# First tokens of a hybrid encoder layer: value, query, key, output and key-query projections with the tokens stationary and 512-column half-row blocks

## The chip, the core and the metric

The kernel runs on one core of a Trainium2 chip. The metric is the device time of one launch in microseconds (us); lower is better. All arithmetic is float32.

## What is computed

One encoder layer over 640 tokens: 512 of one prompt and 8 sequences of 16 sample tokens. D_MODEL is 2048, 1024 channels go to a convolution branch, 16 heads of 64 to attention.

```python
h = rmsnorm(x, norm1_g) * (1 + sc1) + sh1
z = h @ w_in                                  # 2048 -> [GLU value | GLU gate | q | k | v]
u = za * sigmoid(zg)
y_conv = silu(layernorm(causal_dwconv([left, u], w_dw, b_dw)))
o = band_attention(q, k, v)
x = x + g1 * (concat([y_conv, o]) @ w_out)
h2 = rmsnorm(x, norm2_g) * (1 + sc2) + sh2
# PEER: 8 heads, 2 halves each of 128 sub-keys
q = (h2 @ w_pq).reshape(t, 8, 2, 128)
s = einsum('thpd,pnd->thpn', q, sub_keys)     # the "scores" of a head's two halves
sv, si = top_k(s, 16); ...                    # 16 experts for each token and head
u = take(u_experts, eidx);  vv = take(v_experts, eidx)
act = gelu(einsum('td,ted->te', h2, u))       # the "dots"
x = x + g2 * einsum('te,ted->td', g * act, vv)
y = rmsnorm(x, final_g)
```

k and v of the layer are outputs too, in rows of tokens.

## The kernel before

The 640 tokens are 5 tiles of 128. The first two (the "first tokens", `X`, 256 tokens) go ahead alone so that their expert rows can be gathered while the other three (`Y`, 384 tokens) are still in their projections and attention. Every engine has its own program, in the order written in the file; engines wait for each other by semaphores, so what stands behind a wait on an engine waits with it. Nothing is scheduled by a planner.

The stages, in order of time: the modulation vectors (`w_ada`), the GLU columns of all tokens with the depthwise convolution on VectorE (DVE), then for X alone the queries, values and keys (`columns`, L784, and `values_part`, L794), the LayerNorm of the convolution, X's attention (`first_scores`, `first_turn`, `first_weigh`), its output projection (`project_out`, L884), RMSNorm, its key queries and scores (`key_queries`, L913, `key_scores`, L903); then the same for Y from `half_columns` on; and at last the rest of the gathers and a dense product over the value table.

How X's projections are made before: q, k and the key queries have a 128-column block of the weights stationary and stream the 256 tokens (matmuls of 256 columns), so the result has channels on partitions, as attention and the scores want it. v and the output projection have 128 tokens stationary and stream 256 weight columns. Weights come in loads of 256 columns by all 2048 rows (2 MB, rows of 1 KB) into ring slots. ScalarE (ACT) copies each result out of PSUM (`keep_columns`, `keep_values`, L1170 and L1176). For the output k, the kept keys are turned back to token rows in two of the four `rows_out` steps that stand in X's attention loop. The queries are written over the region in which the modulation rows wait to be stored, so ACT waits for that store (`mod_saved`) first.

The kept keys `kT` lie where the convolution's result lies, so they can be copied out only after the 16 Silu operations (L1199) that read it.

What follows the scores: on DVE, `choose(g, k)` (L1662) is the 18-step top-16 selection of head g of a token tile (g = 8 t + h). It waits for the scores of its head. `step(n)` (L1829) is one dot: it waits for gathered row n, runs a multiply-and-sum over 128x2048 (L1853), and interleaves one step of the selection of a head ahead:

```python
for g in range(2):
    for k in range(18):
        choose(g, k)
steps(124)
# in step(n), after the dot, g, s = divmod(n, 16):
if g >= 1 and g + 1 < NG and s < 2 and g + 1 not in (16, 17):
    choose(g + 1, 16 + s)
if g + 2 < NG and g + 2 not in (16, 17):
    choose(g + 2, s)
```

So the first step of head 2's selection stands right behind dot 0, and before dot 1. GpSimd (POOL) issues the gathers (L659), 1 MB each, into four buffers; a buffer is free when its dot is done. After 124 dots DVE turns to Y's attention (first L1914), for which TensorE (PE) waits.

## Time and profile before

| | |
|---|---|
| median of 3 runs | 4143.94 us (4139.81 to 4146.38) |
| the profiled execution's own time | 4143.43 us |
| its span | 4141.7 us |
| mean granted TensorE clock | 0.936 |
| PE / DVE / ACT / POOL busy | 87% / 67% / 11% / 27% |
| bytes moved | 1401.90 MB, mean 338 GB/s |
| X's q, v, k (first matmul to attention) | 510.8 to 717.5 us |
| X's attention | 717.5 to 774.0 us |
| X's output projection | 774.0 to 884.7 us |
| X's key queries | 901.0 to 1050 us |
| first dot, end of the first 124 dots | 950.1, 1371.2 us |

A span runs from the first to the last instruction. Busy shares are averages over stages with different limits; below, single stages are read. A float32 matmul appears in the trace as two records, so "x32" is 16 matmuls.

### The profile page before, as it was taken

What the parts mean: (1) busy time and instruction counts of PE and PEld (TensorE: products, weight loads), DVE (VectorE), ACT (ScalarE), POOL (GpSimd) and SP (SyncE); (2) the same over time, 40 slices, a digit from 0 to 9 for tenths busy, and PEclk for the clock granted to TensorE, in tenths of its full rate; (3) what the DMA queues carried; (4) which work ended last, traced back from release to release, by engine and by line L of the source; (5) the groups of instructions that cost most, each with busy time, mean ns of one, the idle gap of its engine ahead of it and who ended that gap; (6) DMA issues with size and microseconds to landing.
All of it is one profiled execution on the core that took longest, in us unless ns stands there. A gap on an engine that the chain in (4) does not pass through costs nothing.

```text
span 4141.7 us, 34885 instructions
## 1 busy us (share of the span) xinstructions
PE 3599.9 (87%) x12495; PEld 2018.6 (49%) x12495; DVE 2781.5 (67%) x5036; ACT 444.5 (11%) x1084; POOL 1135.5 (27%) x862
## 2 busy tenths in 40 slices
PE   4699989987998689779689999999868999996992
PEld 0466667776553564356534444444353444442441
DVE  2128871227787995679976676676798676655677
ACT  1100002210000230010800000000071000000000
POOL 1100000105554443345043222222404322221233
PEclk8799999998999679889899999999989999998996
DMA  9978743449999999989299999999929999999997
GB/s 351 230 236 259 245 139 130 147 144 380 403 402 413 367 357 335 366 331 397 110 376 417 421 420 409 421 418 421 401 89 374 417 421 421 419 420 397 421 409 304
DMA packets 377072, 1401.90 MB, mean 338 GB/s; under 512 B 22416, under 2 KB 187480, under 8 KB 239653
## 3 DMA queue, kind: packets, MB, share of 16 engines
q0 software_dynamic: 116784, 831.77, 50.4%
q1 hardware_dynamic: 259552, 563.91, 36.9%
q10 hardware_dynamic: 576, 4.19, 0.2%
q8 instruction: 87, 1.43, 0.1%
q14 instruction: 73, 0.60, 0.0%
HBM read 1369.87 MB, written 31.42 MB: 338 GB/s over the span
## 4 chain that ended last, share of the span: by engine, by line
DMA 46%; PE 26%; DVE 12%; issue 11%; POOL 3%; ACT 1%; another core or an unknown queue 0%; SPq 0%; DVEq 0%; POOLq 0%; ACTq 0%
DMA R<-in_u_experts,MS 32%; PE bank L763 10%; DMA R<-in_v_experts,MS 8%; PE bank L945 4%; PE bank L952 3%; DVE R L1763 3%; POOL R L659 3%; PE bank L891 3%; DMA R<-in_w_ada 2%; DVE R L1969 2%; DVE R L1853 1%; PE bank L802 1%; DMA R<-in_w_out 1%; PE bank L717 1%; DVE R L1762 1%
## 5 line engine op out<-in xcount | busy, mean ns | idle before, releaser
L659 POOL DMA_INDIRECT R<-in_u_experts,MS x640 | 931.1, 1455 | 1759.5 <-DVE MS L1853 1475.6
L1853 DVE CUSTOM_DVE_ANT_0 R<-R 128x2048 f32<-128x2048 f32 x368 | 844.4, 2295 | 416.8 <-DMA R<-in_u_experts,MS 404.8
L1118 PE MATMUL bank<-R,RB 128*128 128x512 f32 x2304 | 1019.0, 600 | 75.8 <-DMA R<-in_v_experts 75.7
L1118 PE MATMUL bank<-RB 128*128 128x512 f32 x1792 | 778.2, 592 | 0.0
L1118 PEld LDWEIGHTS bank<-R,RB 128*128 128x128 f32 x2304 | 440.6, 192 | 644.2 <-issue 550.6
L1853 DVE CUSTOM_DVE_ANT_0 R<-R,RB 128x2048 f32<-128x2048 f32 x272 | 622.2, 2287 | 117.5 <-DMA R<-in_u_experts,MS 116.3
L763 PE MATMUL bank<-RB,R 128*128 128x256 f32 (+1 forms) x2048 | 514.0, 412 | 51.4 <-DMA R<-in_w_pq 26.1
L1118 PEld LDWEIGHTS bank<-RB 128*128 128x128 f32 x1792 | 340.5, 190 | 428.6 <-issue 428.6
L763 PEld LDWEIGHTS bank<-RB,R 128*128 128x128 f32 x2048 | 393.1, 193 | 165.7 <-issue 33.9
L1969 DVE SCALAR_TENSOR_TENSOR R<-R,MS 128x2048 f32<-128x2048 f32 x128 | 301.3, 2354 | 183.3 <-DMA R<-in_v_experts,MS 182.0
L945 PE MATMUL bank<-RB,R 128*128 128x384 f32 x1024 | 338.1, 491 | 13.9 <-DMA R<-in_w_in 11.4
L952 PE MATMUL bank<-R,RB 128*128 128x512 f32 x576 | 257.9, 610 | 17.7 <-DMA R<-in_w_out 10.7
L945 PEld LDWEIGHTS bank<-RB,R 128*128 128x128 f32 x1024 | 194.4, 192 | 149.7 <-DMA R<-in_w_in 12.8
L659 POOL DMA_INDIRECT R<-in_v_experts,MS x128 | 154.9, 1210 | 357.6 <-DVE R L1969 328.0
L952 PEld LDWEIGHTS bank<-R,RB 128*128 128x128 f32 x576 | 112.3, 196 | 162.0 <-issue 139.8
L1107 PE MATMUL bank<-R 128*128 128x128 f32 x1024 | 143.8, 292 | 49.1 <-DVE R L1763 22.2
L1546 DVE SCALAR_TENSOR_TENSOR RB<-RB,MS 128x512 f32<-128x512 f32 x240 | 175.8, 732 | 0.0
L694 PE MATMUL bank<-MS,RB 128*128 128x128 f32 (+4 forms) x497 | 84.8, 325 | 87.9 <-DVE RB L1636 21.7
L1107 PEld LDWEIGHTS bank<-R 128*128 128x128 f32 x1024 | 127.4, 198 | 65.9 <-DVE R L1763 45.0
L1465 DVE TENSOR_TENSOR RB<-bank,RB 9x256 f32<-9x256 f32 x128 | 53.5, 418 | 153.4 <-PE bank L717 149.4
L1763 DVE TENSOR_SCALAR R<-MS 128x128 f32<-128x128 f32 x512 | 150.8, 332 | 8.5 <-PE bank L1107 8.5
L694 PEld LDWEIGHTS bank<-MS,RB 128*128 128x128 f32 (+4 forms) x497 | 68.4, 177 | 101.6 <-issue 38.2
(295 smaller groups left out, 2326.7 us busy)
## 6 DMA issues: line engine op xcount, KB each, us to landing
R<-in_v_experts SPq DMA_DIRECT2D x144, 1024.0 KB, 9.1
RB<-in_v_experts SPq DMA_DIRECT2D x112, 1024.0 KB, 9.1
R<-in_w_ada SPq DMA_DIRECT2D x48, 2048.0 KB, 12.8
R<-in_w_in SPq DMA_DIRECT2D x32, 2048.0 KB, 18.5
R<-in_w_out SPq DMA_DIRECT2D x16, 2048.0 KB, 11.5
R<-in_w_pq SPq DMA_DIRECT2D x16, 2048.0 KB, 17.1
R<-in_u_experts,MS POOLq DMA_INDIRECT x640, 11.5
RB<-in_x_prompt POOLq DMA_DIRECT2D x6, 1024.0 KB, 15.0
```

The lines of the kernel that those rows point to most:

```text
L659: pool.indirect_dma_start(dst, None, table, bass.IndirectOffsetOnAxis(ap=expert[T_ % 2][:, c:c + 1], axis=0)).then_inc(signal, 16)
L694: return pe.transpose(out, in_, ident[0:k, 0:k])
L763: m = pe.matmul(PB[2 * par + i][:, 0:src.shape[-1]], w, src[:, k], start=(k == 0), stop=(k == KT - 1))
L891: m = pe.matmul(PB[v % 4][:, 0:BW], src[:, k, t * P:(t + 1) * P], ring[:, j % 2, k, :], start=(k == 0), stop=(k == KT - 1))
L945: m = pe.matmul(PB[bank][:, 0:NY], wide[:, half, i, c * P:(c + 1) * P], src[:, 8 * half + i], start=(half + i == 0), stop=(half + i == 8))
L952: m = pe.matmul(PB[bank][:, :], src[:, 8 * half + i, t * P:(t + 1) * P], wide[:, half, i, :], start=(half + i == 0), stop=(half + i == 8))
L1107: m = pe.matmul(PB[n % 4][:, k * P:(k + 1) * P], oneh[n % 4][:, 1, k], oneh[n % 4][:, 0, k], start=True, stop=True)
L1118: x = pe.matmul(PB[4 * h + q][:, :], W[:, i, h * P:(h + 1) * P], vring[slot][:, q * PW:(q + 1) * PW], start=(i == 0), stop=(i == NKEY - 1))
L1546: ch.mark(STT(out=oP, in0=iP, scalar=w, in1=oP, op0=ALU.mult, op1=ALU.add))
L1763: m = TS(oneh[n % 4][:, 0, k], iota_row, turned[t % 2][:, 0, c:c + 1], turned[t % 2][:, 2, c:c + 1], ALU.is_equal, ALU.mult)
L1853: V.tensor_tensor_reduce(u, u, x, 1.0, 0.0, ALU.mult, ALU.add, dots[t % 2][:, h * TOPK + s:h * TOPK + s + 1]).then_inc(dots_done, 1)
L1969: STT(out=acc, in0=ux[p % NU], scalar=weight[TP][:, p:p + 1], in1=acc, op0=ALU.mult, op1=ALU.add).then_inc(v_used, 1)
```

## The change

X's five projections all get the form that Y's values have already (`half_rows`): 128 tokens stationary, 512 weight columns streamed, weights in half-row loads (1024 rows by 512 columns, again 2 MB, rows of 2 KB). A block of 512 columns takes two loads: both token tiles run on the first, then both on the second. There are `first_rows` for q, v and k, an inline loop for the output and `first_key_queries` for the key queries.

- v comes first, then q, then k. ACT keeps v without waiting for `mod_saved`.
- q and k now come out as token rows, so k needs no turning for its output: the two `rows_out` of k are gone and POOL stores the rows from where ACT put them. q and k are turned to channels by PE (16 transposes each) and copied again by ACT (`turned_rows`). k's turned copies stand behind the 16 Silu.
- The key queries come out as token rows, 2 heads (4 halves) to a 512-column block; they are copied, turned two halves at a time (`turn_queries2`), copied, and scored (`head_scores`). Each load is released half a block at a time.

```diff
@@ SP: loads @@
-            for j in range(NRING):
-                sp.wait_ge(z_done, 16 + 2 * (j + 1))
-                load("w_in", j, 4 * CC + j * BW)
+            x_cols = [(4, 2, 3)[m // 4] * CC + (m // 2 % 2) * PW for m in range(12)]
...
+            for m in range(4, 12):
+                if m % 2 == 0:
+                    sp.wait_ge(w_used, (m - 4) // 2 + 1)
+                else:
+                    sp.wait_ge(z_done, 16 + 2 * ((m - 4) // 2 + 1))
+                load_x_half(m, "w_in", m % 4, x_cols[m])
...
-            for m in range(NPH):
-                if m < 2:
-                    sp.wait_ge(o_done, 14 + 2 * m)
...
-                    sp.wait_ge(q_done, 2 * m - 2)
-                load_pq(m)
+            for m in range(8):
+                if m == 0:
+                    sp.wait_ge(w_used, 10)
+                elif m == 1:
+                    sp.wait_ge(o_done, 8)
+                elif m % 2 == 0:
+                    sp.wait_ge(w_used, 10 + m // 2)
+                else:
+                    sp.wait_ge(q_done, 4 * (m // 2))
+                sp.dma_start(wide[:, m % 2], wv["w_pq"][:, (m % 2) * 8:(m % 2) * 8 + 8, m // 2 * PW:(m // 2 + 1) * PW]).then_inc(w_q[m % 2], 16)
@@ PE: q, v, k @@
-            columns(16, hTX, 4)
-            values_part(24, hTX, 0, TX)
+            for m in range(2):
+                for half in range(2):
+                    first_rows(m, half)
+            first_rows(2, 0)
+            first_rows(2, 1)
+            first_rows(3, 0)
+            pe.wait_ge(mod_free, 4 + NM)
+            turn_queries(0)
+            first_rows(3, 1)
             pe.wait_ge(s_const, 2)
-            pe.wait_ge(mod_free, 4 + NM)
             pe.wait_ge(s_conv, 1)
             channel_sum(4, lambda c: conv_out[:, c], None, None).then_inc(s_mean, 1)
-            values_part(24, hTX, 1, TX)
+            first_rows(4, 0)
+            turn_queries(1)
+            first_rows(4, 1)
+            pe.wait_ge(s_tE, 4)
             channel_sum(6, lambda c: ysq[:, c % 2], s_ysq, s_ysq_used)
-            values_part(24, hTX, 2, TX)
-            values_part(24, hTX, 3, TX)
-            columns(32, hTX, 4)
+            first_rows(5, 0)
+            first_rows(5, 1)
...
-                if h in (3, 6, 9, 12):
+                if h in (3, 6):
                     rows_out(h // 3 - 1)
@@ PE: key queries @@
+            def head_scores(m):
+                for h in range(2):
+                    n = 2 * m + h
+                    pe.wait_ge(q_read, 2 * (n + 1))
+                    if n >= 2:
+                        pe.wait_ge(s_se, 2 * (n - 1))
+                    for t in range(TX):
+                        for p in range(2):
+                            x = pe.matmul(PB[6 + h][:, (2 * t + p) * P:(2 * t + p + 1) * P], q2h[:, h, p, t], skT[:, p],
+                                          start=True, stop=True)
+                    x.then_inc(s_s, 2)
+
+            def first_key_queries():
+                for m in range(4):
+                    for half in range(2):
+                        pe.wait_ge(w_q[half], 16 * (m + 1))
+                        if half == 0 and m >= 2:
+                            pe.wait_ge(s_rE, 2 * (m - 1))
+                        for t in range(TX):
+                            x = half_rows(h2TX, half, half, t, (2 * m + t) % 4)
+                            if half:
+                                x.then_inc(q_done, 2)
+                            elif t == TX - 1:
+                                x.then_inc(w_used, 1)
+                        if half == 0 and m >= 2:
+                            turn_queries2(m - 1)
+                    if m == 0:
+                        turn_queries2(0)
+                        head_scores(0)
+                    elif m >= 2:
+                        head_scores(m - 1)
+                turn_queries2(3)
+                head_scores(3)
@@ ACT @@
+            act.wait_ge(s_u, 8)
+            for v in range(4):
+                keep_columns(16 + v, vst[v])
             act.wait_ge(mod_saved, 16)
...
+            for t in range(TX):
+                keep_columns(26 + t, ost[:, t, PW:2 * PW])
             for c in range(CT):
                 act.wait_ge(s_lnx, c + 1)
...
             act.wait_ge(s_cat, CT)
-            for c in range(CT):
-                keep_columns(32 + c, kT[:, c, 0:NX])
+            for u in range(4):
+                turned_rows(4 + u, kT[:, 4 * (u // 2):4 * (u // 2) + 4])
```

The other lines renumber semaphore counts. DVE's program is the same but for the residual of X, which now has 8 pairs of operations on 512 columns in place of 16 on 256.

PE at X's key queries, before. L763 is the projection (x32 is two 128-column blocks, both halves of one head), L909 the scores.

```order
L694 MATMUL bank<-MS,RB 128x128 x32
L763 MATMUL bank<-RB,R 128x256 x32
L909 MATMUL bank<-MS 128x128 x4
L763 MATMUL bank<-RB,R 128x256 x32
L909 MATMUL bank<-MS 128x128 x2
L763 MATMUL bank<-RB,R 128x256 x16
```

The same place in the changed kernel. L808 is `half_rows`, L715 a transpose, L966 the scores of two heads.

```order
L715 MATMUL bank<-MS,RB 128x128 x32
L808 MATMUL bank<-R,RB 128x512 x32
L715 MATMUL bank<-MS,RB 128x128 x8
L966 MATMUL bank<-MS 128x128 x8
L808 MATMUL bank<-R,RB 128x512 x48
L715 MATMUL bank<-MS,RB 128x128 x8
L808 MATMUL bank<-R,RB 128x512 x16
L966 MATMUL bank<-MS 128x128 x8
```

Before, a half's scores follow one block of 16 matmuls behind its projection. Now the scores of heads 2 and 3 follow 64 matmuls of 512 columns and 8 transposes behind those of heads 0 and 1.

ACT between the last squares of the LayerNorm and X's attention, before. L1199 is Silu (16 of them), L1170 the copies of k, L1220 the first exponential. The 14 further Silu rows, which alternate in the same way, are left out.

```order
L1176 ACTIVATE MS<-bank 128x256 x4
L1199 ACT_TABLE_LOAD
L1199 ACTIVATE RB<-RB,MS 128x256
L1199 ACTIVATE RB<-RB,MS 128x384
...
L1170 ACTIVATE RB<-bank 128x256 x8
L1220 ACT_TABLE_LOAD
```

The same piece now. L1236 copies k's rows (these two are its last block), L1275 is Silu, L1241 the turned copies.

```order
L1236 ACTIVATE RB<-bank 128x512 x2
L1275 ACT_TABLE_LOAD
L1275 ACTIVATE RB<-RB,MS 128x256
L1275 ACTIVATE RB<-RB,MS 128x384
...
L1241 ACTIVATE RB<-bank 128x4x128 x4
L1298 ACT_TABLE_LOAD
```

Before, Silu stood ahead of all eight copies of k and ran beside its matmuls. Now it stands behind the copy of k's last block, and the turned copies, for which attention waits, behind Silu.

## Rows read from the trace of the kernel before

**Rows 1.** Timeline of PE, 500 to 720 us: start, us, engine, line, [idle before <-releaser].

```profile
510.83 14.08 PE L763 MATMUL bank<-RB,R 128*128 128x256 f32 x64
...
543.75 43.83 PE L763 MATMUL bank<-RB,R 128*128 128x256 f32 x192 [18.84 <-ACT RB L1170]
...
601.24 1.02 PE L810 MATMUL bank<-RB,MS 128*128 128x512 f32 x2
...
609.89 13.98 PE L802 MATMUL bank<-R,RB 128*128 128x256 f32 x64
...
717.54 0.71 PE L850 MATMUL bank<-RB 64*128 64x256 f32 x4 [0.56 <-ACT RB L1170]
```

**Rows 2.** Timeline of ACT, 500 to 960 us.

```profile
543.23 0.66 ACT L1170 ACTIVATE RB<-bank 128x256 f32<-128x256 f32 x2 [35.09 <-DMA mod_scratch<-RB]
...
662.16 1.28 ACT L1199 ACT_TABLE_LOAD   x1
...
663.46 8.82 ACT L1199 ACTIVATE RB<-RB,MS 128x256 f32<-128x256 f32 x16
...
898.85 2.06 ACT L1259 ACTIVATE RB<-bank 128x512 f32<-128x512 f32 x4 [2.55 <-PE bank L694]
```

**Rows 3.** Timeline of DVE, 608 to 620 us.

```profile
610.09 0.69 DVE L1571 TENSOR_TENSOR RB<-RB,bank 128x512 f32<-128x512 f32 x1 [16.58 <-PE bank L811]
```

**Rows 4.** Timeline of PE in X's attention and at the output projection.

```profile
738.49 0.70 PE L850 MATMUL bank<-RB 64*128 64x256 f32 x2
...
742.25 0.70 PE L850 MATMUL bank<-RB 64*128 64x256 f32 x2
...
745.14 0.70 PE L850 MATMUL bank<-RB 64*128 64x256 f32 x2
...
773.98 110.75 PE L891 MATMUL bank<-R,RB 128*128 128x256 f32 x512 [0.52 <-issue]
```

**Rows 5.** Timeline of PE in Y's values: 24 matmuls of 512 columns.

```profile
1311.33 20.87 PE L952 MATMUL bank<-R,RB 128*128 128x512 f32 x48 [1.26 <-DMA R<-in_w_in]
```

**Rows 6.** Timeline of PE, 880 to 1400 us: X's key queries, Y's attention.

```profile
900.97 14.08 PE L763 MATMUL bank<-RB,R 128*128 128x256 f32 x64 [0.84 <-ACT RB L1259]
...
990.28 9.62 PE L763 MATMUL bank<-RB,R 128*128 128x256 f32 x32 [15.67 <-DMA R<-in_w_pq]
...
1373.00 3.78 PE L1007 MATMUL bank<-RB 64*128 64x128 f32 x16 [37.04 <-DVE RB L1914]
```

**Rows 7.** Timeline of DVE, 880 to 1100 us: residual, selection, first dots.

```profile
884.76 0.42 DVE L1620 TENSOR_TENSOR MS<-bank,R 128x256 f32<-128x256 f32 x1 [6.02 <-PE bank L891]
...
938.41 0.49 DVE L1683 MAX8 MS<-RB 128x8 f32<-128x128 f32 x2 [2.99 <-ACT RB L1265]
...
950.07 2.28 DVE L1853 CUSTOM_DVE_ANT_0 R<-R,RB 128x2048 f32<-128x2048 f32 x1
...
953.12 0.49 DVE L1683 MAX8 MS<-RB 128x8 f32<-128x128 f32 x2 [0.76 <-ACT RB L1265]
...
953.52 2.27 DVE L1853 CUSTOM_DVE_ANT_0 R<-R,RB 128x2048 f32<-128x2048 f32 x1
```

**Rows 8.** L393 (w_pq loads), issue at 944.8, then issue at 959.5: time to landing.

```profile
DMA to landing us min/median/max: 12.0/12.0/12.0
...
DMA to landing us min/median/max: 30.7/30.7/30.7
```

**Rows 9.** L332 (weight loads), issues from 420 to 900 us: time to landing.

```profile
DMA to landing us min/median/max: 7.9/8.5/18.3
```

**Rows 10.** Stretches: us, PE PEld DVE ACT POOL busy, PEclk, DMA share, GB/s.

```profile
953.50:1371.20 417.70, 334.57 (x1066) 202.31 (x1064) 337.37 (x545) 24.37 (x50) 229.54 (x123) 0.91 1.01 402
...
2100.00:2900.00 800.00, 783.92 (x1807) 344.32 (x1806) 554.83 (x892) 6.06 (x7) 226.44 (x201) 0.99 1.01 418
```

**Rows 11.** Waits of DVE, 953.5 to 1371.2 us: total, times, longest.

```profile
DVE R L1853 <- DMA R<-in_u_experts,MS: 77.8, 86, 4.3
```

**Rows 12.** L659 (gathers) in Y's attention, 1378 to 1567 us: time to landing.

```profile
DMA to landing us min/median/max: 6.0/9.0/10.3
```

More of the change, by code:

```diff
@@ L381, in _ @@
                 first_bias(h)
-            for j in range(2):
-                sp.wait_ge(z_done, 32 + 2 * (j + 1))
-                load("w_out", j, j * BW)
+            sp.wait_ge(w_used, 5)
+            load_x_half(0, "w_out", 0, 0)
+            sp.wait_ge(z_done, 26)
+            load_x_half(1, "w_out", 1, 0)
             for h in range(4, NH):
@@ L929, in _ @@
             pe.wait_ge(s_cat, CT)
             pe.wait_ge(pv_read, NH)
-            for j in range(8):
-                project_out(0, j, catX, TX)
-            pe.wait_ge(o_free, 4 + 16)
+            for j in range(4):
+                for half in range(2):
+                    weights_in(half)
+                    for t in range(TX):
+                        v = TX * j + t
+                        if half == 0:
+                            pe.wait_ge(o_free, v + 1)
+                        m = half_rows(catX, half, half, t, v % 4)
+                        if half:
+                            m.then_inc(o_done, 1)
+                        elif t == TX - 1:
+                            m.then_inc(w_used, 1)
@@ L934, in _ @@
+            pe.wait_ge(o_free, 4 + 8)
             pe.wait_ge(s_sq, T + TX)
@@ L947, in half_columns @@
                 return m
-            def half_rows(src, half, t, bank):
-                for i in range(8):
-                    m = pe.matmul(PB[bank][:, :], src[:, 8 * half + i, t * P:(t + 1) * P], wide[:, half, i, :],
-                                  start=(half + i == 0), stop=(half + i == 8))
-                return m
             for b in range(4):
@@ L974, in _ @@
                     for t in range(TY):
-                        m = half_rows(hTY, half, t, TY * j + t)
+                        m = half_rows(hTY, half, half, t, TY * j + t)
                         if half:
@@ L1265, in keep_scores, with keep_rows2, keep_turned2, keep_head_scores @@
                 A(dst[:, 0:tiles, n], PB[4 + 2 * b][:, 0:tiles * P].rearrange("p (t n) -> p t n", t=tiles), ACT.Copy).then_inc(s_se, 1)
+            def keep_rows2(m):
+                for t in range(TX):
+                    act.wait_ge(q_done, 4 * m + 2 * t + 2)
+                    if m >= 2:
+                        act.wait_ge(s_tT, 8 + 2 * (m - 1))
+                    A(qrows[:, m % 2, t], PB[(2 * m + t) % 4][:, :], ACT.Copy).then_inc(s_rE, 1)
+            def keep_turned2(m):
+                for h in range(2):
+                    n = 2 * m + h
+                    act.wait_ge(s_tT, 8 + n + 1)
+                    if n >= 2:
+                        act.wait_ge(s_s, 2 * (n - 1))
+                    A(q2h[:, h], PB[4 + h][:, :].rearrange("p (i t n) -> p i t n", i=2, t=TX), ACT.Copy).then_inc(q_read, 2)
+            def keep_head_scores(m):
+                for h in range(2):
+                    n = 2 * m + h
+                    act.wait_ge(s_s, 2 * (n + 1))
+                    A(SX[:, :, 2 * n:2 * n + 2], PB[6 + h][:, :].rearrange("p (t i n) -> p t i n", t=TX, i=2), ACT.Copy).then_inc(s_se, 2)
+            def keep_first_queries():
+                keep_rows2(0)
+                keep_turned2(0)
+                keep_head_scores(0)
+                keep_rows2(1)
+                for m in range(1, 4):
+                    keep_turned2(m)
+                    if m < 3:
+                        keep_rows2(m + 1)
+                    keep_head_scores(m)
             def keep_queries(G, dst, tiles):
@@ L1640, in _ @@
             for i in range(4):
-                dve.wait_ge(s_vst[i], 16 * 2)
-            for v in range(8 * TX):
+                dve.wait_ge(s_vst[i], 16)
+            for v in range(4 * TX):
                 j, t = divmod(v, TX)
```

263 lines of the change are left out of this document (141 added, 122 removed).

## The prediction

> **What bounds the kernel now.** I read the chain of waits first. From X's key queries on it runs over DVE and the gathers for 400 us, then Y's attention, then to the end. So two questions matter: when do the dots start, and how fast do they run. The timeline of DVE gives the start: dot 0 at 950.07, then head 2's selection at 953.12, dot 1 at 953.52 [rows 7]. The stretch of dots 1 to 123 takes 417.7 us at 402 GB/s, with a DMA share of 1.01 [rows 10]. DVE waits for gathers for only 77.8 us of it [rows 11]; without them it would take 339.9 us. PE waits 37.04 us for DVE at Y's attention [rows 6]: up to there PE has slack and DVE has none. All later stages follow DVE's 124th dot one to one: 48 dots stand in Y's attention, where they never wait, and what follows is in the same order as before. So the sum is the shift of the start of Y's attention on DVE, now 1371.2.
>
> Before the dots, 510 to 950 us, PE bounds. It idles 18.84 us at 524.9 [rows 1], since ACT waits until 543.23 for the modulation store [rows 2].
>
> **Streaming.** 512 columns bring PE nothing: 24 matmuls of 512 take 20.87 us, 0.870 each [rows 5]; 256 matmuls of 256 take 110.75, 0.433 each [rows 4]. Half the matmuls at twice the price. A half-row load is 16 matmuls (two tiles), 13.91 us. X's q, v and k have 12 of these, the output projection 8, the key queries 8.
>
> **From 510.83 to X's attention.** v runs first and is not held, so the 18.84 us go. PE: v 4 x 13.91 to 566.5; q's first three 41.7 to 608.2; 8 transposes (0.87, which is what a head with a turning group costs above one without, 3.76 - 2.89 [rows 4]); q's last 13.91 to 623.0. The convolution is done by then: DVE had been idle for 16.58 us at 610.09, since 593.5 [rows 3]. Channel sum 8.65 (601.24 to 609.89 [rows 1]) to 631.7; k's first block with 8 transposes 28.7 to 660.4; second channel sum 8.65 to 669.0; k's second block 27.8 to 696.9. A weight load lands in 8.5 us (at most 18.3) [rows 9] and has 13.9 us or more; the one issued at 507 beside two others is needed at 524.7, as before. I cost the loads at nothing; their cover is those 13.9 us.
>
> Here ACT is late next. Behind k's last copy (0.6) come the Silu table and the 16 Silu, 1.28 + 8.82, which lay beside k's matmuls before [rows 2], then 4 turned copies, 2.06 for four of that size [rows 2]. PE's 16 transposes lie beside them. Attention can start at 696.9 + 12.8 = 709.7, where it started at 717.54 [rows 1]: -7.8 us. The 18.84 us are given back in part to three terms: 12.8 behind k, 1.7 for q's transposes, and 0.09 for each load.
>
> **X's attention** loses two turning groups: -1.7. PE comes to it after 13 us with no matmul but the transposes. After an idle of 15.67 us, 16 key-query matmuls took 9.62 us instead of 7.04 [rows 6]. Attention is not PE's to set, so between 0 and +2.6 I take +1. The output projection then starts at 765.4 (before 773.98). It takes 111.3 for 110.75, to 876.7. The last residual has two operations on 512 columns, 0.69 each [rows 3], where it had 0.42 [rows 7]: +0.5. Norm, transposes and copies are unchanged, 884.73 to 900.97, 16.24. Key queries start at 893.5, 7.5 us early.
>
> **Scores of heads 0 and 1.** Block 0 takes 27.8 + 0.3 to 921.6; copy 0.6, transposes 0.9, copies, scores and copies some 2.3. Both heads' scores are there at about 925. Selection 0 is free at once. One selection takes 11.7 us (938.41 to 950.07 [rows 7]); two take it to 948.3. Dot 0 starts about 2 us earlier than before.
>
> **Scores of heads 2 and 3: the new wait.** Selection 2 stands between dot 0 and dot 1. Its scores come behind 64 matmuls of 512, no longer behind 32 of 256. PE goes on at 924.3; block 1 to 952.1; the first half of block 2 needs a load issued at 938 beside the first four gathers. The nearest rows are 12.0 us to landing (few gathers about) and 30.7 (the dots at full rate) [rows 8]. Against 13.9 that is a stall of 0 to 17. Since DVE issues only one gather more before it waits, it is nearest to the first; four gathers and the load are 6.3 MB, at 402 GB/s 15.7 us, so I take +2. The Trainium skill, "DMA: Bandwidth & Descriptors", Queues, rings and completion order, says an engine takes turns between its queues packet by packet. By that the load would have half the rate and land in 10.4 us, and the sum would be 2 lower. Block 2 then ends at 954.1 + 13.9 + 0.9 + 13.9 = 982.8; scores and copies 1.2: 984.0. Dot 1 starts at 984.4, where it started at 953.5: +30.9 us.
>
> **What of that comes back.** While DVE waits, only PE's loads move. At dot 1 before, the key-query loads for blocks 5 to 7 and a rest of the fourth were still to come, 3.3; now only the last one has, since PE has run on without its stalls of 15.67 and so on [rows 6]. 2.3 loads of 2.1 MB are 4.8 MB; the stretch had 417.7 x 402 = 167.9 MB to move, now 163.1. At 402 GB/s that is 405.7 us, against 417.7: -12. Dot 124 ends at 1390.1. The bounds: at the 418 GB/s of the later stage with 8 KB rows [rows 10] it is 390.2, a shift of +3.4; by DVE alone 339.9 [rows 11], if transfers were no bound at all. I take 402, since the same weight loads share this stretch; they end some 27 us earlier than before, but from there DVE's own 339.9 / 123 = 2.76 us a dot and up leaves little to catch up.
>
> PE's other gains do not count. It finishes Y's values some 27 us earlier, and waits for DVE 87 instead of 37.
>
> Sum: -7.8 - 0.7 (attention) + 0.6 + 0.5 brings the key queries 7.5 earlier; the start of dot 1 is +30.9; the stretch gives back 12: **+19 us**. On the profiled execution's 4143.4 that is 4162.4; it lies 0.5 below the median of the runs, so the forecast is 4162.5.
>
> **The rivals.**
>
> *A. The wait is mostly made up.* If the stretch can move 418 GB/s once DVE comes in refreshed and the weight loads thin out, the shift is +3.4, 4147. For it: the same engines do 418 later. Against: there all rows are 8 KB, here 17 weight loads (a fifth of the bytes) have rows of 1 or 2 KB. Chance 0.15.
>
> *B. More goes wrong ahead of the scores.* The load for block 2 lands like the 30.7 us one: 17 instead of 2, so +15 more; or ACT holds X's q copies, and the early 7.5 us are lost. Price +27 to +42: 4171 to 4185. Against: DVE is waiting, so no gathers crowd the load. Chance 0.11.
>
> *C. Faster.* The stretch is not bound by bytes, but by the loop of four buffers: landing, dot, issue. In Y's attention, with few weight loads about, gathers land in 9.0 us in the median [rows 12]. Then a loop is 9.0 + 2.3 for the dot + 0.9 for the issue, 12.2 us for four dots, 3.05 a dot; 123 of them take 375 us. Place: dots 1 to 123. From 984.4 they end at 1359.6, a shift of -11.6: 4132. It decides for faster once a dot takes under 3.07 us; before it took 3.40. For it: DVE waits in only 77.8 of 417.7 us. Against: a DMA share of 1.01, and the 9.0 us come from a stage with 48 dots in 195 us, a third fewer gathers in the air. The Trainium skill, same page, Where 436 GB/s comes from, has 435 GB/s as the ceiling; at that 163.1 MB would take 375 us, the same answer. No stretch here shows more than 418. Chance 0.09.
>
> That the change does not do what it says is excluded by the order: no engine schedules itself.
>
> **How the numbers follow.** The forecast (shift +9 to +27, 4152 to 4170) has 0.65, A 0.15, B 0.11, C 0.09. What a measurement of this kernel can tell from no change is 0.2%, 8.3 us: 4135.7 to 4152.2. Slower: 0.65 + 0.11 = 0.76; within: A, 0.15; faster: C, 0.09. Range 4146 to 4178: the forecast, most of A and half of B, 0.82.
>
> **What would show it.** Right: PE without the wait at 525; attention of X about 8 us earlier, with ACT's Silu right ahead of it; key queries near 893; the first step of selection 2 waiting about 31 us for ACT's score copy, with dot 0 near 948 and dot 1 near 984; hardly a stall for w_pq loads; PE's wait for DVE at Y's attention about 87 us; Y's attention at about 1390. Wrong: a wait ahead of selection 2 under 15 us, or dots 1 to 123 in under 395 us.

## The result and the profile after

The change makes the kernel slower, by 0.6 to 1%. Four runs of it have a median of 4189.91 us (4173.62 to 4196.73), four of the kernel before 4141.88 us (4139.69 to 4146.38): ratio 1.0097, 95% interval 1.0078 to 1.0117. The direction was forecast; the size was not, +48 us against the +19 of the forecast, and the result lies outside the range. Seven more runs of the same kernel in a later set have a median of 4172.19 us (4166.74 to 4187.92) against 4148.19: ratio 1.0062 (1.0039 to 1.0085), +24 us. So this kernel's own time varies by 30 us, and what it varies by is part of the answer. Two profiled executions of the changed kernel are read here: execution one, 4191.98 us, and execution two, 4169.90 us, from the later set.

Timeline of PE in execution one (columns as in [rows 1]):

```profile
512.76 96.40 PE L808 MATMUL bank<-R,RB 128*128 128x512 f32 x224
...
710.10 1.23 PE L894 MATMUL bank<-RB 64*128 64x256 f32 x4 [11.26 <-ACT RB L1241]
...
781.27 112.27 PE L808 MATMUL bank<-R,RB 128*128 128x512 f32 x256 [0.51 <-issue]
...
911.28 29.73 PE L808 MATMUL bank<-R,RB 128*128 128x512 f32 x64 [0.69 <-ACT RB L1337]
...
976.59 15.70 PE L808 MATMUL bank<-R,RB 128*128 128x512 f32 x32 [3.90 <-DMA R<-in_w_pq]
...
1418.68 3.78 PE L1073 MATMUL bank<-RB 64*128 64x128 f32 x16 [81.41 <-DVE RB L2024]
```

The wait of 18.84 us of [rows 1] is gone: 224 records follow one another from 512.76 on. X's attention starts 7.4 us earlier than before, but the output projection behind it starts 7.3 us later (before 773.98 [rows 4]). Y's attention starts 45.7 us later, after a wait for DVE of 81.41 instead of 37.04 us [rows 6].

ACT ahead of X's attention, the same execution:

```profile
697.13 0.60 ACT L1236 ACTIVATE RB<-bank 128x512 f32<-128x512 f32 x1 [6.27 <-PE bank L808]
697.74 1.28 ACT L1275 ACT_TABLE_LOAD   x1
699.04 8.82 ACT L1275 ACTIVATE RB<-RB,MS 128x256 f32<-128x256 f32 x16
707.89 2.07 ACT L1241 ACTIVATE RB<-bank 128x512 f32<-128x512 f32 x4
```

That is the 12.8 us of work the prediction put there. DVE, at the rows that answer to [rows 7]:

```profile
945.17 0.49 DVE L1793 MAX8 MS<-RB 128x8 f32<-128x128 f32 x2 [33.44 <-ACT RB L1364]
...
968.02 2.29 DVE L1963 CUSTOM_DVE_ANT_0 R<-R,RB 128x2048 f32<-128x2048 f32 x1
...
1008.63 0.49 DVE L1793 MAX8 MS<-RB 128x8 f32<-128x128 f32 x2 [38.31 <-ACT RB L1364]
1009.03 2.27 DVE L1963 CUSTOM_DVE_ANT_0 R<-R,RB 128x2048 f32<-128x2048 f32 x1
```

Head 2's selection waits 38.31 us for the score copy where it waited 0.76 us. Dots 1 to 123 and the attention of X as stretches (columns as in [rows 10]):

```profile
710.10:781.27 71.17, 65.11 (x192) 40.46 (x193) 21.48 (x127) 32.06 (x101) 8.93 (x16) 0.50 0.21 66
...
1009.03:1417.20 408.17, 296.48 (x854) 158.72 (x852) 336.90 (x547) 23.05 (x42) 219.81 (x122) 0.87 1.01 400
```

408.2 us at 400 GB/s are 163.3 MB, against 163.1 forecast. The new thing is in the first row: the granted clock is 0.50, its lower level (1.2 GHz), through all of X's attention. A head takes 3.97 us. In the kernel before only the third and fourth head start at that price, and from the fifth on a head takes 2.89 us (3.76 with a turning group). The starts of scores of the third, fourth and fifth head (the row of four records ahead of them is the first two heads, every further row one):

```profile
723.26 1.22 PE L850 MATMUL bank<-RB 64*128 64x256 f32 x2
...
727.24 1.22 PE L850 MATMUL bank<-RB 64*128 64x256 f32 x2
...
732.71 0.70 PE L850 MATMUL bank<-RB 64*128 64x256 f32 x2
```

Execution two of the changed kernel has the same 11.26 us wait ahead of attention as execution one, and yet:

```profile
708.45:764.47 56.02, 41.82 (x192) 27.55 (x193) 21.50 (x127) 32.07 (x101) 8.96 (x16) 0.85 0.26 83
988.60:1395.10 406.50, 295.62 (x854) 158.34 (x852) 336.82 (x547) 23.15 (x42) 226.60 (x122) 0.87 1.01 402
```

Here the clock came back at about 725 us, behind the first four heads, as in the kernel before at about 732 us. Attention takes 56.0 us, 15.2 fewer. The starts side by side, in us:

| | before | forecast | execution two | execution one |
|---|---|---|---|---|
| X's attention | 717.54 | 709.7 | 708.45 | 710.10 |
| X's output projection | 773.98 | 765.4 | 764.47 | 781.27 |
| key queries | 900.97 | 893.5 | 892.65 | 911.28 |
| selection 0 | 923.98 | 925 | 924.53 | 945.17 |
| dot 0 | 950.07 | 948.3 | 947.40 | 968.02 |
| dot 1 | 953.52 | 984.4 | 988.70 | 1009.03 |
| Y's attention on PE | 1373.00 | 1391.9 | 1396.58 | 1418.68 |
| span | 4141.7 | 4160.7 | 4168.1 | 4190.2 |

(1391.9 is the shift of 18.9 us on 1373.00, and 4160.7 is 4141.7 + 19.)

### The profile page after: what moved, and what is told of

Same layout as the page of the kernel before. It is cut to its first block, busy times and chain, and to the rows that moved or that the text cites. A ratio compares the mean times of both kernels' runs of the same rounds, so it can differ in the third digit from the quotient of the medians.

```text
span 4190.2 us, 33145 instructions
## 1 busy us (share of the span) xinstructions
PE 3625.8 (87%) x11647; PEld 1864.1 (44%) x11647; DVE 2777.6 (66%) x5020; ACT 446.5 (11%) x1069; POOL 1114.0 (27%) x858
## 4 chain that ended last, share of the span: by engine, by line
DMA 47%; PE 24%; issue 13%; DVE 11%; POOL 3%; ACT 1%; another core or an unknown queue 0%; SPq 0%; DVEq 0%; POOLq 0%; ACTq 0%
DMA R<-in_u_experts,MS 34%; PE bank L808 11%; DMA R<-in_v_experts,MS 8%; PE bank L784 7%; POOL R L680 3%; DVE R L1873 3%; DMA R<-in_w_ada 2%; DVE R L2079 2%; DVE R L1963 2%; PE bank L738 1%; DVE R L1872 1%; DMA R<-in_w_out 1%; PE bank L715 1%; PE bank L1073 0%; DMA R<-in_w_pq 0%
## 5 line engine op out<-in xcount | busy, mean ns | idle before, releaser
L680 POOL DMA_INDIRECT R<-in_u_experts,MS x640 | 910.4, 1422 | 1816.4 <-DVE MS L1963 1525.8
L1184 PE MATMUL bank<-R,RB 128*128 128x512 f32 x2304 | 1019.2, 600 | 81.0 <-DMA R<-in_v_experts 80.8
L1184 PEld LDWEIGHTS bank<-R,RB 128*128 128x128 f32 x2304 | 440.6, 192 | 649.6 <-issue 549.5
L808 PE MATMUL bank<-R,RB 128*128 128x512 f32 x1472 | 650.5, 604 | 27.8 <-DMA R<-in_w_in 13.9
L808 PEld LDWEIGHTS bank<-R,RB 128*128 128x128 f32 x1472 | 284.0, 194 | 385.9 <-issue 353.0
L784 PE MATMUL bank<-RB,R 128*128 128x256 f32 (+1 forms) x1024 | 282.3, 437 | 5.6 <-DVE RB L1625 5.6
L1018 PEld LDWEIGHTS bank<-RB,R 128*128 128x128 f32 x1024 | 194.4, 191 | 149.5 <-DMA R<-in_w_in 14.8
L784 PEld LDWEIGHTS bank<-RB,R 128*128 128x128 f32 x1024 | 194.8, 192 | 90.3 <-issue 13.6
L715 PE MATMUL bank<-MS,RB 128*128 128x128 f32 (+3 forms) x561 | 95.2, 322 | 96.3 <-DVE RB L1860 24.4
L715 PEld LDWEIGHTS bank<-MS,RB 128*128 128x128 f32 (+3 forms) x561 | 75.5, 173 | 117.2 <-issue 43.8
```

The source lines that it names most:

```text
L680: pool.indirect_dma_start(dst, None, table, bass.IndirectOffsetOnAxis(ap=expert[T_ % 2][:, c:c + 1], axis=0)).then_inc(signal, 16)
L715: return pe.transpose(out, in_, ident[0:k, 0:k])
L784: m = pe.matmul(PB[2 * par + i][:, 0:src.shape[-1]], w, src[:, k], start=(k == 0), stop=(k == KT - 1))
L808: m = pe.matmul(PB[bank][:, :], src[:, 8 * half + i, t * P:(t + 1) * P], wide[:, slot, i, :], start=(half + i == 0), stop=(half + i == 8))
L1018: m = pe.matmul(PB[bank][:, 0:NY], wide[:, half, i, c * P:(c + 1) * P], src[:, 8 * half + i], start=(half + i == 0), stop=(half + i == 8))
L1184: x = pe.matmul(PB[4 * h + q][:, :], W[:, i, h * P:(h + 1) * P], vring[slot][:, q * PW:(q + 1) * PW], start=(i == 0), stop=(i == NKEY - 1))
```

## The experiments

Two theories stood after the first trace. **One:** the score wait (64 matmuls of 512 ahead of the scores of heads 2 and 3) costs what was forecast, and the rest is the clock in X's attention. **Two:** the rest comes from the changed streaming or the loads in v, q, k and the output projection. All experiments edit the changed kernel, save the one that moves attention in the kernel before. They were run in three sets, each with its own runs of the kernel before, whose medians are 4147.47, 4148.19 and 4148.72 us. Every version has one profiled execution. Up to the end of X's attention the versions "key queries of before", "scores of block 1 at once" and "head 2's selection deferred" are the changed kernel unchanged.

**The key queries of before.** Only the key queries (with their loads, copies and scores) go back; v, q, k and the output projection stay as changed.

```diff
-            first_key_queries()
+            key_queries(0, h2TX, TX)
```

> The changed kernel with the key queries of X as they were before the change (weights stationary, 256-column loads, a head's scores one block behind), all else changed. Theory 1: the key queries start where they start now, 911, which is 10 us later than before the change, and from there everything runs as before: dot 0 near 960, dot 1 near 964, 26.7 us of stalls for w_pq loads, Y's attention near 1383, the kernel 10 us above the kernel before, 4152. So of the 48 us lost some 38 are the key queries' part. Rival: the key queries cost nothing by themselves, and the loss is all in the slow attention and what it shifts (17 us) and in contention: then the time stays above 4180.

Measured: 4148.55 us (4129.87 to 4162.79, 10 runs), ratio 0.9999 (0.9979 to 1.0019). Five runs lie at 4130 to 4145 and five at 4153 to 4163 us. The profiled one belongs to the second five, and shows the lower clock to the end of attention (us, PE busy, PEclk, DMA share, GB/s):

```profile
710.00:720.00 10.00, 6.01 (x21) 0.50 0.41 156
...
740.00:760.00 20.00, 19.88 (x57) 0.50 0.31 78
```

The forecast was 4152 us. So the loss on the median belongs to the key queries, and the first half of the change is worth nothing on the median: what it gains in half of the runs, it loses in the others, where the mean clock is lower (0.924 to 0.930, against 0.934 to 0.936). That all five kept the lower level through attention is read from one of them. Theory two falls.

**Scores of block 1 at once.** The queries of block 1 are turned and scored behind block 1 instead of behind the first half of block 2; ACT's copies move along.

```diff
-                        if half == 0 and m >= 2:
-                            turn_queries2(m - 1)
-                    if m == 0:
-                        turn_queries2(0)
-                        head_scores(0)
-                    elif m >= 2:
-                        head_scores(m - 1)
+                        if half == 0 and m == 3:
+                            turn_queries2(2)
+                    if m < 2:
+                        turn_queries2(m)
+                        head_scores(m)
+                    elif m == 3:
+                        head_scores(2)
```

> The changed kernel with the key queries of block 1 (heads 2 and 3) turned and scored right behind that block, as block 0's are, instead of one block later. Theory 1: DVE's wait ahead of head 2's selection (38.3 us) is a cost of the order alone. It falls to about 6 us, dot 1 starts about 32 us earlier (near 977 instead of 1009), and since fewer weight loads have been done by then, 9 to 12 us are given back in the stretch of dots 1 to 123; Y's attention starts 20 to 24 us earlier, and the kernel takes about 4168. Rival: the stretch is bound by bytes from the first dot on and all of the wait is made up, so that Y's attention starts at the same time within 5 us, and the kernel takes 4186 to 4191.

Measured: 4144.22 us (4134.86 to 4168.00, 10 runs), ratio 1.0001 (0.9979 to 1.0023), 28 us under the changed kernel's 4172.19. Seven runs lie at 4134.9 to 4145.0 us with clocks of 0.932 to 0.938, three at 4162.7 to 4168.0 with 0.924 to 0.928: two groups here too. DVE waits for head 2's scores (first row below) far less than 38.31 us:

```profile
955.25 0.49 DVE L1794 MAX8 MS<-RB 128x8 f32<-128x128 f32 x2 [6.49 <-ACT RB L1364]
```

On PE:

```profile
707.52 1.23 PE L894 MATMUL bank<-RB 64*128 64x256 f32 x4 [11.26 <-ACT RB L1241]
...
1368.45 3.78 PE L1073 MATMUL bank<-RB 64*128 64x128 f32 x16 [38.65 <-DVE RB L2025]
```

Y's attention starts 28.1 us earlier than in execution two (forecast 20 to 24 against execution one). Both executions had the recovered clock, and selection 0 starts within 0.9 us of the same time, so this is the price of where the scores stand.

**Head 2's selection deferred.** Nothing moves on PE; DVE no longer stands behind the wait.

```diff
+                if g == 0:
+                    if s >= 8:
+                        choose(2, 2 * s - 16)
+                        choose(2, 2 * s - 15)
-                if g + 2 < NG and g + 2 not in (16, 17):
+                elif g + 2 < NG and g + 2 not in (16, 17):
                     choose(g + 2, s)
```

> The changed kernel with one edit on DVE: the sixteen pieces of head 2's selection stand two by two behind dots 8 to 15 instead of one by one behind dots 0 to 15, so that dots 1 to 7 no longer stand behind its wait for the scores. Theory (the score wait stops the weight gathers through their buffers): selection 0 still starts some 21 us later than before, the scores of head 2 still come at about 1008 us in an execution with the low clock in attention, but dots 1 to 7 (3.3 us each) run in that wait, and the attention of Y starts some 20 to 24 us earlier than in the changed kernel: about 1396 us with the low clock in the first tokens' attention and 1380 us with the recovered one; median about 4167 us. Rival (the gathers are late by the start of selection 0 and 1 alone, or by another queue): Y's attention starts as late as in the changed kernel, median 4185 to 4190 us.

Measured: 4152.97 us (4140.40 to 4177.58, 10 runs), ratio 1.0018 (0.9997 to 1.0039). The expected median of 4167 us was reckoned from 4185; from the 4172.19 of the same set the gain is 19 us. The profiled execution had the lower clock throughout attention, as execution one had:

```profile
942.91 0.49 DVE L1793 MAX8 MS<-RB 128x8 f32<-128x128 f32 x2 [33.51 <-ACT RB L1364]
...
1007.97 0.49 DVE L1793 MAX8 MS<-RB 128x8 f32<-128x128 f32 x2 [14.31 <-ACT RB L1364]
```

```profile
1396.79 3.78 PE L1073 MATMUL bank<-RB 64*128 64x128 f32 x16 [60.53 <-DVE RB L2028]
```

The scores are as late as in execution one (1008.63), but the wait is 24.0 us shorter, and Y's attention starts 21.9 us earlier, 2.3 of which come from an earlier start of selection 0. So late scores cost less by themselves than through what stands behind them: the dots, and with them the buffers of the gathers.

**Silu first.** The 16 Silu go ahead of the copy of k's last block on ACT, so that PE's last 32 matmuls hide them.

```diff
-            for t in range(TX):
-                keep_columns(26 + t, ost[:, t, PW:2 * PW])
             for c in range(CT):
                 act.wait_ge(s_lnx, c + 1)
                 ...
                 m.then_inc(s_cat, 1)
+            for t in range(TX):
+                keep_columns(26 + t, ost[:, t, PW:2 * PW])
```

> The changed kernel with its 16 Silu on ACT moved ahead of the copy of k's last block, so that they run beside that block's matmuls. Two theories on X's attention, which took 71.2 us here (3.97 us a head) and 56.4 before (2.89 a head). Theory 1: TensorE's clock is at its lower level for the whole attention because PE stands idle for 11.3 us right ahead of it, while ACT does Silu. Then attention starts about 10 us earlier (700 instead of 710), a head takes 2.89 us again after the first few, and the output projection starts 24 to 26 us earlier, near 756; the kernel takes about 4165 us. Rival: the clock is low because attention has two turning groups less, whatever stands ahead of it. Then a head still takes 3.97, only the 10 us are won, and the kernel takes about 4181.

Measured: 4167.30 us (4150.19 to 4184.99, 8 runs), ratio 1.0054 (1.0034 to 1.0074). PE at the scores of the first four heads:

```profile
698.42 0.71 PE L894 MATMUL bank<-RB 64*128 64x256 f32 x4 [1.00 <-ACT RB L1241]
704.15 1.22 PE L894 MATMUL bank<-RB 64*128 64x256 f32 x2
708.12 1.22 PE L894 MATMUL bank<-RB 64*128 64x256 f32 x2
```

The wait of 11.26 us is 1.00. Y's attention starts at 1388.72, 7.9 us ahead of execution two's. But two of the eight runs still took 4184 and 4185 us, with mean granted clocks of 0.925 and 0.920 against 0.929 to 0.933 in the others. If these two kept the lower clock through attention (they have no profile), the idle ahead of attention is not what decides whether the clock comes back.

**The wait filled.** The same wait holds 26 matmuls of 256 columns (output used nowhere).

```diff
+            pe.wait_ge(z_free, 2 + 28)
+            for i in range(26):
+                pe.matmul(PB[0][:, 0:2 * P], ident, skT.rearrange("p h n -> p (h n)"), start=True, stop=True)
             pe.wait_ge(s_tE, 8)
```

> The changed kernel with 26 matmuls of 256 columns more, identity by the sub-keys into a free PSUM bank, in the 11.3 us in which PE waits for ACT ahead of X's attention; their result is not used. Theory 1 (the idle stretch drops TensorE's clock, and attention does not bring it back): attention starts at the same time within 1.5 us, takes 56 to 58 us instead of 71.2, and the kernel takes about 4176. Rival (attention's own light load keeps the clock low): 3.97 us a head as before, and the same time or 1 us more, 4191.

Measured: 4170.76 us (4164.59 to 4193.56, 5 runs), ratio 1.0069 (1.0040 to 1.0098). PE at the scores of the first three heads and of the fifth:

```profile
708.98 0.71 PE L897 MATMUL bank<-RB 64*128 64x256 f32 x4
...
714.73 1.22 PE L897 MATMUL bank<-RB 64*128 64x256 f32 x2
...
724.02 0.70 PE L897 MATMUL bank<-RB 64*128 64x256 f32 x2
```

PE enters attention at the full clock, which is at the lower level 5.8 us later and back at 724 us; Y's attention starts at 1395.82, as in execution two. One of the five runs, 4193.56 us at a clock of 0.923, looks like execution one. A busy PE ahead of attention buys nothing here: without the idle, the clock falls in the attention itself.

**The changed kernel once more**, for its spread.

> The changed kernel itself, unedited. What decides its spread: if the first tokens' attention runs its 16 heads either at the lower clock throughout (71 us) or with three heads only at it (55 us), the times fall into two groups about 16 us apart, near 4173 and near 4190 us, as the four runs so far have it (4173.6 against 4187.9 to 4196.7); the rival is one broad group. No change in the median of about 4185 us.

Measured: 4166.74, 4167.56, 4169.90, 4172.19, 4174.03, 4179.88 and 4187.92 us. The last, with the lowest clock (0.922), falls where execution one is. Of eleven runs, four lie at 4187.9 to 4196.7 us with clocks of 0.922 to 0.924, seven at 4166.7 to 4179.9 with 0.928 to 0.934. My expectation of a median of 4185 us missed: the first four runs had held three with the lower clock.

**More columns in attention.** Two matmuls of 256 columns more in ten of the 16 heads, where PE waits for DVE anyway.

```diff
+                if h == 9:
+                    pe.wait_ge(s_oE, 2)
+                if 1 <= h <= 2 or 9 <= h <= NH:
+                    for i in range(2):
+                        pe.matmul(PB[6][:, i * 256:i * 256 + 256], ident, skT.rearrange("p h n -> p (h n)"), start=True, stop=True)
                 if 1 <= h <= NH:
                     first_turn(h - 1)
```

> The changed kernel with two matmuls of 256 columns more in 10 of the 16 heads of the first tokens' attention, ahead of the turn for which TensorE waits 0.70 us a head at the full clock (their output is used nowhere). Theory (attention is so light on TensorE that the clock falls in it, and it comes back by chance): more columns bring the clock back after about three heads in all or nearly all executions, at little cost at the full clock, attention some 56 to 60 us, and the times lie in one group near 4173 us. Rival (the load has nothing to do with it): as many executions as without them stay at the lower clock, where each pair costs 0.87 us, 10 heads 8.7 us, so one group near 4198 us and another near 4175 us.

Measured: 4175.74 us (4173.28 to 4184.49, 6 runs), ratio 1.0063 (1.0042 to 1.0085): a single group 11 us wide. With four in eleven at the lower clock, six without one would come by chance 7 times in 100, so this alone does not settle it. The time does not tell it either: the profiled execution is the slowest, 4184.49 us, and yet its clock was back by the fifth head (724.85 us). Nor is the version faster: its median is 3.6 us above that of the changed kernel in the same set. (A pair is 0.87 us at the full clock, not at the lower one as I had written; a head with a pair takes 3.03 instead of 2.89 us.)

**The same columns with the key queries of before.**

> The changed kernel with the key queries of before, and the same extra matmuls in attention. Without them 5 of 10 executions lay at 4130 to 4145 us and 5 at 4153 to 4163 us. Theory: one group at 4132 to 4148 us, about 3 us above the lower group for the extra matmuls' own time. Rival: two groups as without them.

Measured: 4146.25 us (4138.47 to 4153.90, 11 runs), ratio 0.9995 (0.9985 to 1.0004). Of the ten runs without the columns five lay at 4152.6 us or above, of these eleven one (4153.90, at a clock of 0.934), with two more at 4151.5; the spread is 15 us instead of 33. Five of the eleven lie above the 4132 to 4148 us of the forecast. In the profiled execution the clock is back by the third head, at 716.5 us, a little short of full in places (0.94):

```profile
710.00:720.00 10.00, 7.65 (x27) 0.67 0.56 219
720.00:730.00 10.00, 8.07 (x43) 0.94 0.20 52
...
740.00:760.00 20.00, 20.00 (x101) 1.00 0.21 58
```

The median gains only 2.3 us, though: the group lies 9 us above the lower half of the version without the columns (mean 4137.4). The extra matmuls explain about 1.4 of them (ten heads by 0.14); the rest is not explained.

**The kernel before, attention moved.** 24 matmuls of 256 columns ahead of X's attention in the kernel before.

> The kernel before with 24 matmuls of 256 columns (0.216 us each, 5.2 us, TensorE busy, output used nowhere) ahead of the first tokens' attention, which moves it from 717.5 to about 722.7 us. Asked: is it the changed kernel's stage of v, q and k, or only the time at which attention begins, that lets the clock stay low in some executions? If it is only the phase: some executions of this one also keep the low clock through attention, two groups some 16 us apart, near 4149 and 4165 us. If it is the stage ahead: one group as for the kernel before, median about 4152 us, which is 4147 us and the 5 us added.

Measured: 4157.73 us (4150.93 to 4168.29, 11 runs), ratio 1.0020 (1.0009 to 1.0031).

```profile
717.90 10.60 PE L844 MATMUL bank<-MS 128*128 128x256 f32 x48 [0.56 <-ACT RB L1172]
728.42 0.71 PE L852 MATMUL bank<-RB 64*128 64x256 f32 x4
```

24 matmuls are 48 records of 0.22 us, so the shift was 10.9 us, not 5.2. The median went up by 9.0, which the shift accounts for. Four of the eleven runs lie at 4163 to 4168 us, 4 us above the next, but with clocks of 0.931 to 0.932, within the 0.929 to 0.938 of the kernel before. So moving attention in time shows no clear second group, and eleven runs do not exclude one; the profiled execution is the second shortest.

**All three moves, then with the columns.** Silu first, block 1's scores at once, head 2's selection deferred:

> The changed kernel with three edits together: Silu ahead of the copy of k's last block on ACT, block 1's queries turned and scored right behind block 1, and the deferral of head 2's selection. If the three waits are separate, their gains add as far as they stand on one path: selection 0 starts some 10 us earlier than before (about 913 us), and nothing waits in front of dot 1, so Y's attention starts about 1356 to 1362 us against 1373 before; median 4128 to 4138 us, faster than both kernels. Rival (the stage of dots is then bound by something that these edits do not move, such as the start of the weight gathers, or the low clock in attention returns in most executions): 4140 us or more.

Measured: 4141.07 us (4122.44 to 4157.12, 12 runs), ratio 0.9987 (0.9967 to 1.0008). DVE reaches dot 1 with no wait for scores, and Y's attention starts within the forecast 1356 to 1362:

```profile
1357.40 3.78 PE L1073 MATMUL bank<-RB 64*128 64x128 f32 x16 [50.76 <-DVE RB L2029]
```

The median missed by 3 us and falls on the rival's side (4140 or more): five of the twelve runs lie at 4150 to 4157 us, with clocks of 0.926 to 0.931. None of the five has a profile.

> The version with all three moves (Silu ahead of the copy of k's last block, block 1's scores right behind block 1, head 2's selection deferred) and the extra matmuls in 10 heads of the first tokens' attention (two of 256 columns each, output used nowhere). Theory (the extra columns keep the chip from leaving TensorE at the lower clock for the whole of attention): one group of times at 4125 to 4145 us, median about 4136 us, none near 4155 us, where 5 of 12 executions without the extra matmuls lay (4150 to 4157 us). Rival (the six executions with them that agreed did so by chance): the same two groups, a third or more of the executions at 4155 us and above, median 4143 us or more.

Measured: 4132.42 us (4119.55 to 4145.98, 7 runs), ratio 0.9964 (0.9950 to 0.9977). This version beats both kernels: 16 us under the kernel before. Against the version without the columns it is 9 us faster in the medians, though the intervals of the two ratios overlap. Its PE is at the full clock at the third head's scores (0.70 us, not 1.22; the fourth takes 0.80):

```profile
697.63 0.71 PE L894 MATMUL bank<-RB 64*128 64x256 f32 x4 [1.00 <-ACT RB L1246]
702.99 0.70 PE L894 MATMUL bank<-RB 64*128 64x256 f32 x2
...
1354.25 3.78 PE L1078 MATMUL bank<-RB 64*128 64x128 f32 x16 [27.69 <-DVE RB L2034]
```

Over the three versions with the columns, 24 runs, the times of each spread over 11, 15 and 26 us; the same versions without them spread over 30, 33 and 35 us, with 4 of 11, 5 of 10 and 5 of 12 runs in what looks like an upper group. The borders of these groups are drawn by eye (in the 26 us one run, 4145.98, stands 11 us above the next), and in the medians the columns are worth +3.6, -2.3 and -8.7 us.

**From selection 0 to Y's attention.** The distance between these two starts in the profiled executions leaves out all that the clock did in X's attention, and shows what the key queries, the selections and the dots take:

| | selection 0 | Y's attention on PE | between |
|---|---|---|---|
| kernel before | 923.98 | 1373.00 | 449.0 |
| kernel before, attention moved | 934.83 | 1383.24 | 448.4 |
| changed kernel, execution one | 945.17 | 1418.68 | 473.5 |
| changed kernel, execution two | 924.53 | 1396.58 | 472.1 |
| Silu first | 913.16 | 1388.72 | 475.6 |
| the wait filled | 923.78 | 1395.82 | 472.0 |
| more columns in attention | 928.89 | 1399.71 | 470.8 |
| key queries of before | 935.18 | 1377.35 | 442.2 |
| scores of block 1 at once | 923.63 | 1368.45 | 444.8 |
| head 2's selection deferred | 942.91 | 1396.79 | 453.9 |
| all three moves | 911.85 | 1357.40 | 445.6 |
| all three moves, with the columns | 914.55 | 1354.25 | 439.7 |

All five executions in which the key queries and the selection are those of the change lie at 471 to 476 us, whatever the clock did ahead of them, 22 to 27 above the kernel before. Moving block 1's scores takes all of that away, deferring the selection four fifths of it.

## Why the prediction was right and wrong

**Right: the start of X's attention.** The step "attention can start at 696.9 + 12.8 = 709.7" measured 710.10 and 708.45. The weight loads cost nothing, and the 12.8 us are ACT's last copy, Silu with its table, and the turned copies. With the Silu first the wait is 1.00 us.

**Wrong: "Attention is not PE's to set, so between 0 and +2.6 I take +1."** This term of the sum was mis-sized, and its upper bound was as well. It is the step that failed, by 15.5 us where the clock stays low. In execution two it holds (56.0 us, forecast 55.7). In execution one attention takes 71.2 us, 15.5 over the forecast. The reason given was false: at the lower clock the row 710.10:781.27 has PE busy for 65.11 of 71.17 us, so there it is PE's to set, at 3.97 us a head. [rows 4] has only rows at the full clock, and [rows 6] bounded one block of key queries. The price of a head at the lower level stood in the trace of before (3.98 us from 723.26 to 727.24). The bound had to be the 12 heads behind the first four by 1.08 us, 13 us, and some 2 us for a turning group and the last heads' turns and products: one execution in which the clock came back does not say that it must. With the 15.5 the sum is 4178, the upper end of the range.

That is still 12 us short of the median of 4189.91. Execution one's span ends 29.5 us behind the forecast: 20.2 are there at selection 0 (15.5 of them attention; the output projection takes 112.27 instead of 111.3, as the granted clock is still 0.72 from 780 to 790 us, and block 0 of the key queries 29.73 instead of 28.1), 4.5 more come at dot 1, 2.1 between dot 1 and Y's attention, and 2.7 behind it. Execution two is 7.4 behind the forecast, with nothing from attention.

**Right, somewhat short: the score wait.** "Dot 1 starts at 984.4" measured 988.70 in execution two. The wait ahead of head 2's selection, forecast at about 31 us, is 38.3 and 38.6. Of the 4.3 us, 2.2 are the stall for block 2's load (4.2 instead of the 2 taken) and 1.8 the half block behind it (15.70 instead of 13.9). The stall itself speaks against the shorter landing: the load was issued at 938.4 us and PE went on at 956.25, 17.9 us later (17.6 in execution one). The Trainium skill, "DMA: Bandwidth & Descriptors", Queues, rings and completion order, has an engine take turns between its queues packet by packet. From it the prediction took half the rate and an estimate of 10.4 us; this trace does not agree with the estimate, and is nearer to the 15.7 us that the load and the gathers beside it take one after the other. Two edits confirm the mechanism: scores moved, Y's attention 28 us earlier; selection deferred, 22 us earlier with scores as late as ever.

**Right: what comes back.** 405.7 us forecast for dots 1 to 123; 406.5 and 408.2 measured, at 402 and 400 GB/s. In execution two Y's attention is 23.6 us later than before, where the sum had 18.9.

**The rivals.** A (418 GB/s) and C (the loop of buffers) did not occur. B's price, 4171 to 4185, is the nearest of the three to what was measured, but that is luck: it rested on a stall of 17 us, which was 3.9 and 4.2, or on a loss of the early 7.5 us ahead of attention, and attention did start as early as forecast.

**The spread.** Of the seven runs at 4167 to 4180 us six lie within the range of 4146 to 4178. The four others don't, and the range had no case for them. What follows Y's attention adds its own: the distance from its start to the end is 2768.7 us before, 2771.5 in both executions of the changed kernel, and from 2759.7 to 2784.4 in the experiments, whose edits lie ahead of it. What moves it is not known, so a difference of some 10 us between two profiled executions should be read at Y's attention and not at the end.

**Open.** With v, q and k changed, the lower clock lasts through attention in a part of the runs. The kernel before shows no such group: of its 73 runs beside the experiments one is at 4166.6 us with a clock of 0.929, the others are at 4135.4 to 4160.1 us. The filled or removed wait and the moved start did not decide it. With the extra columns no run looks like execution one, which speaks for too little work for TensorE in attention, but this is argued and not shown. The change takes two turning groups out of attention, behind the scores of the tenth and the thirteenth head. They cannot be why the clock stayed low up to there: to that point both kernels have the same matmuls in attention, and in the kernel before the clock was back at 732.71 us, at the fifth head, while execution one kept the lower level through all of them. Why one execution of the same program gets it back and another does not is open.

## What to carry to other kernels

An engine that waits in line between two of its own pieces of work (here DVE, for scores, between two dots) stops everything that its progress frees (here the buffers of the gathers); ask first whether that wait can stand later in its program, before making the producer faster. When a stage becomes light for TensorE, bound its time by every row of it at the lower clock, not by one block, and take several executions: a single profile cannot show that there are two groups. A few matmuls placed where TensorE waits anyway narrowed the spread in all three versions in which they were tried, but they lowered the median clearly in none.

## What was not expected

The same program took attention at 3.97 us a head in one execution and at 2.89 in another, behind the same 11.26 us wait. Where TensorE is busy up to attention, the clock falls about 5 us into it (in the kernel before, and with the 26 matmuls more); in the changed kernel it has fallen already in the wait ahead of it, at about 704 us:

```profile
702.00:704.00 2.00, 0.00 (x0) 0.93 1.00 250
704.00:706.00 2.00, 0.00 (x0) 0.50 1.01 426
```

At the lower level the records of attention fill 91% of the stretch (65.11 of 71.17 us) and in execution two 75% (41.82 of 56.02), so the clock stayed low in the execution in which TensorE's records filled more of the stretch. Of the three profiled executions with the extra matmuls in attention, two were at the full clock at the third head's scores (0.70 us and not 1.22), the one without the 11.26 us wait and the one with the key queries of before. The other was not (1.22 us at the third and fourth head), though up to the end of attention it runs the same program as the one with the key queries of before.
